# Gates of the attention heads: the sigmoid as exp(-ln(1 + exp(-x))) on ScalarE, the sum and the reciprocal on VectorE dropped

## The reference, cut to what matters

```
for layer in range(DEPTH):                       # DEPTH = 2
    h = rms_norm(x, norm_g[layer])
    proj = einsum('btd,dc->btc', h, w_in[layer])
    sb_q, sb_k, sb_v, sb_g, mb_q, mb_k, mb_v, mb_g, mem_q, mem_g = split(proj)
    o_sb  = merge_heads(stick_breaking_attention(...)) * silu(sb_g)    # 6 heads of 64
    o_mb  = merge_heads(moba_attention(...))           * silu(mb_g)    # 6 heads of 64
    o_mem = merge_heads(memory_attention(...))         * silu(mem_g)   # 4 heads of 64
    x = x + einsum('btc,cd->btd', concatenate([o_sb, o_mb, o_mem]), w_out[layer])
```

## Time and profile before

| | |
|---|---|
| three runs | 875.87, 870.71, 875.02 us |
| the profiled execution | 871.39 us |
| its span, first to last instruction | 869.5 us |
| TensorE (matmul) busy | 822.5 us, 95% |
| VectorE busy | 550.7 us, 63% |
| ScalarE busy | 471.6 us, 54% |
| GpSimd busy | 128.1 us, 15% |
| mean granted TensorE clock | 0.98 of full speed |

### The profile page before, as it was taken

One profiled execution on the slowest core, in us unless ns is written; L12 is line 12 of the kernel. 1 busy time (PEld: TensorE's weight loads), 2 busy tenths in 40 slices (PEclk: granted clock), 3 DMA queues, 4 the chain that ended last, 5 costly groups with the idle time before them and its releaser, 6 DMA issues.

```text
span 869.5 us, 12747 instructions
## 1 busy us (share of the span) xinstructions
PE 822.5 (95%) x4238; PEld 667.5 (77%) x4238; DVE 550.7 (63%) x797; ACT 471.6 (54%) x970; POOL 128.1 (15%) x205
## 2 busy tenths in 40 slices
PE   8998999999999999789998999999998999999996
PEld 5877877777776787587777888788886788888885
DVE  5567576676777776766665566666576455455444
ACT  5665665466775554645565656564546444344343
POOL 2100021000232210153323442200000000000000
PEclk9999999999999999998999999999999999999999
DMA  8964543366676454642223344456664556646641
GB/s 253 272 161 143 143 151 119 97 194 195 201 221 178 136 163 114 193 128 83 82 74 89 107 133 139 146 149 229 199 196 148 167 181 191 211 153 196 206 147 49
DMA packets 147454, 137.78 MB, mean 158 GB/s; under 512 B 15184, under 2 KB 115808, under 8 KB 147392
## 3 DMA queue, kind: packets, MB, share of 16 engines
q1 hardware_dynamic: 145296, 129.89, 49.4%
q0 software_dynamic: 2096, 7.09, 2.8%
HBM read 135.90 MB, written 1.05 MB: 157 GB/s over the span
## 4 chain that ended last, share of the span: by engine, by line
PE 73%; ACT 6%; DVE 4%; issue 2%; ACTq 0%; DVEq 0%
PE psum L1095 58%; PE psum L1061 6%; PE psum L1178 3%; PE psum L1313 2%; PE psum L1085 2%; ACT w_hi L1355 2%; ACT probs L1480 2%; PE psum L1281 1%; DVE w_lo L1548 1%; ACT p_t L1498 1%; DVE stats L1681 0%; PE psum L1239 0%; ACT gtmp L1523 0%; DVE x L1581 0%; ACT p_t L1366 0%
## 5 line engine op out<-in xcount | busy, mean ns | idle before, releaser
L1548 DVE TENSOR_TENSOR w_lo<-raw,w_hi 128x1024 fp32r<-128x1024 f32 (+1 forms) x254 | 296.7, 1184 | 134.5 <-ACT w_hi L1355 81.2
L1355 ACT ACTIVATE w_hi<-raw 128x1024 fp32r<-128x1024 f32 (+1 forms) x254 | 252.9, 1016 | 68.3 <-PE psum L1095 50.7
L1095 PE MATMUL psum<-w_hi,h_hi 128*128 128x512 f32 (+1 forms) x656 | 261.4, 398 | 10.3 <-DVE h_lo L1602 9.3
L1095 PE MATMUL psum<-w_lo,h_hi 128*128 128x512 f32 (+1 forms) x656 | 249.1, 380 | 0.0
L1095 PE MATMUL psum<-w_hi,h_lo 128*128 128x512 f32 (+1 forms) x656 | 248.7, 379 | 0.0
L1095 PEld LDWEIGHTS psum<-w_hi,h_hi 128*128 128x128 f32 x656 | 125.5, 191 | 35.6 <-issue 13.6
L1095 PEld LDWEIGHTS psum<-w_lo,h_hi 128*128 128x128 f32 x656 | 125.3, 191 | 19.6
L1095 PEld LDWEIGHTS psum<-w_hi,h_lo 128*128 128x128 f32 x656 | 125.9, 192 | 16.1
L1480 ACT ACTIVATE probs<-psum,stats 128x272 f32<-128x272 f32 (+2 forms) x104 | 47.3, 464 | 64.2 <-DVE stats L1673 27.9
L1095 PE MATMUL psum<-w_hi,m_hi 128*128 128x512 f32 x152 | 60.2, 396 | 2.4 <-DVE m_lo L1602 1.7
L1095 PE MATMUL psum<-w_lo,m_hi 128*128 128x512 f32 x152 | 59.3, 390 | 0.0
(11 more groups left out here) (175 smaller groups left out, 1042.0 us busy)
## 6 DMA issues: line engine op xcount, KB each, us to landing
raw<-in_w_in SPq DMA_DIRECT2D x112, 256.0 KB, 3.5
raw<-in_w_in SPq DMA_DIRECT2D x44, 512.0 KB, 4.3
raw<-in_w_ffn_in SPq DMA_DIRECT2D x88, 256.0 KB, 3.8
raw<-in_w_out SPq DMA_DIRECT2D x24, 512.0 KB, 3.3
raw<-in_w_in SPq DMA_DIRECT2D x64, 192.0 KB, 2.7
raw<-in_w_ffn_out SPq DMA_DIRECT2D x22, 512.0 KB, 4.6
raw<-in_w_mem_kv SPq DMA_DIRECT2D x8, 512.0 KB, 3.9
raw<-in_w_branch_swa SPq DMA_DIRECT2D x8, 512.0 KB, 3.4
```

The lines of the kernel that those rows point to most:

```text
L1095: last = nc.tensor.matmul(psum[:, bank, 0:n], sx[name][:, c, t * P:(t + 1) * P], wx[:, u["slot"], kk, 0:n], start=u["first"] and kk == 0 a ...
L1355: nc.scalar.activation(w_hi[:, u["slot"], :, 0:n], raw[:, u["raw"], :, 0:n], ACT.Copy)\
L1548: nc.vector.tensor_tensor(w_lo[:, u["slot"], :, 0:n], raw[:, u["raw"], :, 0:n], w_hi[:, u["slot"], :, 0:n].bitcast(F32), ALU.subtract)\
```

## The change

ScalarE now computes the whole sigmoid: exp(-x), then ln(1 + that) in place, then exp of its negative in place. The first two are each waited for by ScalarE before it issues the next. The signal `gate_e` moves to the third. VectorE is left with the multiplication by x. Semaphores, their counts, the order of steps and all else stay.

```diff
@@ ScalarE, step "gate"
                         act.wait_ge(gate_done, s["before"])
-                    nc.scalar.activation(gtmp[:, t, 0:gw], stage[:, g["ga"] % NSTAGE, t, c0:c0 + gw], ACT.Exp,
-                                         scale=-1.0).then_inc(gate_e, 1)
+                    gt = gtmp[:, t, 0:gw]
+                    link(nc.scalar.activation(gt, stage[:, g["ga"] % NSTAGE, t, c0:c0 + gw], ACT.Exp, scale=-1.0))
+                    link(nc.scalar.activation(gt, gt, ACT.Ln, bias=1.0))
+                    nc.scalar.activation(gt, gt, ACT.Exp, scale=-1.0).then_inc(gate_e, 1)
@@ VectorE, step "gate"
                     dve.wait_ge(gate_e, s["n"] + 1)
-
-                    gt = gtmp[:, t, 0:gw]
-                    link(nc.vector.tensor_scalar(gt, gt, 1.0, None, ALU.add))
-                    link(nc.vector.reciprocal(gt, gt))
-                    nc.vector.tensor_tensor(sgate[:, g["ga"] % 2, t, 0:gw], gt,
+                    nc.vector.tensor_tensor(sgate[:, g["ga"] % 2, t, 0:gw], gtmp[:, t, 0:gw],
                                             stage[:, g["ga"] % NSTAGE, t, c0:c0 + gw],
                                             ALU.mult).then_inc(gate_done, 1)
```

## The result

The full change was measured three times, each time beside the kernel before on the same chip:

| comparison | before, median (runs) | changed, median (runs) | ratio, 95% interval |
|---|---|---|---|
| first | 872.57 us (7) | 865.40 us (7) | 0.991, 0.9887 to 0.9934 |
| second (e12) | 874.91 us (25) | 867.21 us (6) | 0.9915, 0.9883 to 0.9946 |
| third (e16) | 873.54 us (23) | 865.40 us (6) | 0.991, 0.9883 to 0.9938 |

The account below looks back on a forecast made before the run. TensorE was taken to bound the kernel; waits of -1.64, -0.5 and -0.14 us and a clock drop of -1.7 us made -4.0 us, from a median of 875.02 to 871.0 us. Forecast 867 to 873 us, full range 865.5 to 877.5 us.

Parts of the forecast that it names:

- TensorE bounds the kernel, and only its waits can be given back: Between 30 and 338 us TensorE is busy 295.8 of 308 us, so at most 12.2 us can be given back directly.
- What leaves VectorE and what comes to ScalarE: Over 28 gates, additions and reciprocals of 37.3 us leave VectorE, and two more activations per gate bring ScalarE 19.9 us.
- ScalarE's side costs nothing: At the 28 gates, ScalarE's added 0.68 or 0.90 us each is covered by idle time and split-weight margins: 0 us.
- The wait until 266.35 and the clock drop behind it: TensorE's wait behind a 256-wide gate goes wholly, -1.64 us, and the half-clock stretch from 267.6 us with it, -1.7 us.
- next late is nothing near: After the wait until 266.35 goes, the high half behind the gate moves to 262.2, its unit unused until 272.8.
- The wait until 127.65: The chain behind the 256-wide gate at 116.92 to 119.49 starts earlier: -0.5 us, bounds 0 and -0.6.
- The wait until 70.66: TensorE's 2.28 us wait is set by ScalarE, despite two gates on VectorE ahead of it: -0.14 us.
- the sum: Gates between 30 and 336 us: three shorter waits give -2.3 us, with the clock drop -4.0 us.
- Nothing moves: The wait until 266.35 becomes another, or the clock drops elsewhere: 0 to -1.5 us, 873.5 to 875 us; chance 0.25.
- ScalarE becomes late: At gates without ScalarE idle time behind them, the added work reaches TensorE: slower, 878.5 us; chance 0.10.
- The tables are reloaded: On ScalarE each gate loads tables twice for ln and exp, 71.8 us; kernel near 900 us or more; chance 0.01.
- VectorE was late throughout: All eleven TensorE waits between 30 and 338 us, 12.2 us, and two clock drops go: 859.4 us; chance 0.07.

Follow-up runs that it names:

- e12: The full change, unchanged, for a second profile and more runs; 867.21 us, ratio to before 0.9915.
- e16: The full change, unchanged, measured beside the kernel of e15 on the same chip; 865.40 us, ratio to before 0.991.
- e2: Only the 24 128-wide gates computed on ScalarE, the four 256-wide as in the kernel before; 873.93 us, ratio to before 1.0002.
- e3: Kernel before with VectorE's addition and reciprocal left out and nothing added on ScalarE; 865.99 us, ratio to before 0.992.
- e4: Kernel before with the three activations on ScalarE, VectorE keeping addition, reciprocal and product; 877.16 us, ratio to before 1.0041.
- e9: Kernel before with one gate on ScalarE, the 256-wide one ahead of the wait until 266 us; 870.89 us, ratio 0.9961.
- e5: The kernel before, unchanged, for a second profile; 874.52 us, ratio to itself 1.0019.
- e6: Kernel before with only the first four gates, all 128 wide, computed on ScalarE; 872.65 us, ratio to before 0.9988.
- e10: The full change except the 256-wide gate ahead of the wait until 266 us, which stays on VectorE; 869.46 us, ratio to before 0.9944.
- e14: Kernel before with one gate on ScalarE, the 256-wide one at 116 us; 873.60 us, ratio to before 0.9998.
- e7: Kernel before with the four 256-wide and the first four narrow gates on ScalarE; 865.16 us, ratio to before 0.9919.
- e8: The full change plus the second pair of layer 0 memory transposes one unit earlier; 863.67 us, ratio to before 0.9899.
- e15: Same kernel as e8, measured again beside the unchanged full change on one chip; 864.82 us, ratio to before 0.9901.
- e11: The full change for all gates except the first four, which stay as before; 869.12 us, ratio to before 0.9933.
- e1: Kernel before with only the four 256-wide gates computed on ScalarE; 869.38 us, ratio to before 0.9959.
- e13: Kernel before with five gates on ScalarE, the first four and the 256-wide one ahead of the wait until 266 us; 869.25 us, ratio 0.9952.

## Why the prediction was right or wrong, point by point

**TensorE bounds the kernel, and only its waits can be given back: right.** VectorE lost 35 us and the kernel 7.7. With the waits moves the clock, on which more below. The 24 narrow gates, 29 us of VectorE's work (24 x 1.2), are worth nothing by themselves (e2: 1.0002).

**What leaves VectorE and what comes to ScalarE: right.** 37.3 and 19.9 us were forecast; in the window from 30 to 338 us VectorE is 32.9 us less busy and ScalarE 17.9 more. A little more of the program fits into the window after. The new rows add up to 15.0 us at 128 columns and 3.4 at 256, 18.4 us; the forecast's 19.9 has the links in it, in which the engine is not busy.

**ScalarE's side costs nothing: right as far as the times tell, but not for the reason given.** e3, without ScalarE's work, is no faster than the full change; its profile has 0.58 and 0.35 us less of two waits, so in the trace the added work is not quite free. The cover named was ScalarE's idle time and the margins of the split weights. e4 has both, adds the same work and is 3.6 us slower: the cover that counts is the work which VectorE no longer has behind the same gate.

**The wait until 266.35 and the clock drop behind it, -1.64 and -1.7 us: right that both go, and in part luck that their sum fits.** e9 changes that gate alone and gains 3.4 us (1.7 to 5.2 us) where the two terms make 3.3. In 18 profiles, seven have the wait (the first of before, e2, e4, e5, e6, e10, e14), each with one or two drops that begin between 266 and 274 us; eleven do not have it, and none of them has a drop between 262 and 280 us. Three of those (the first of after, e7, e12) have one at 284 to 286 us instead, behind waits that stayed there. So the drop goes with its wait, and can come back at a later one. The first profile of after is such a case. Windows, columns as in the earlier trace rows, of after and then of before:

```profile
284.50:287.90 3.40, 3.40 (x11) 2.74 (x11) 2.01 (x7) 0.53 (x2) 0.00 (x0) 0.50 0.81 224
```

```profile
465.60:469.00 3.40, 3.40 (x13) 2.96 (x11) 0.96 (x1) 1.93 (x3) 0.00 (x0) 0.50 0.02 5
```

Between 30 and 338 us both first profiles have two drops of 3.4 us, which the prediction had named as a sign of being wrong; the drop that after has fewer is the one at 465.6 us, where the change touches nothing. That the profiled execution came near the sum is therefore luck in its clock term. Nor is "next late is nothing near" right: TensorE's next wait, which ends between 279 and 293 us, is 0.27 to 0.30 us in five of the seven profiles with the drop at 266 to 274 us (0.53 and 0.99 in e6 and e4), and 0.63 to 0.99 us in ten of the eleven without (0.30 in e3).

**The wait until 127.65, -0.5 us: right in kind.** It is 0.74 us shorter in the full change, a little beyond the bound of 0.6, and 0.4 us by its own gate (e14).

**The wait until 70.66, -0.14 us: right.** 0.12 us. That the order sets it and not the gates held in e8 and e15.

**The step that failed is the sum, -2.3 us of waits and -1.7 us of clock.** It was made on one profiled execution and carried over to the median of the runs as it stood. It put the gates of 30 to 50 us at nothing, without a reason, and these carry a wait of 0.27 to 1.28 us in five of seven profiles. And it counted one clock drop of 1.7 us, where the runs show 4.6 us less withheld. These two are shown; how the whole 7.7 us divide is not.

*The missing term is the first four gates.* I said nothing of 30 to 50 us, since TensorE had no wait there in the one profile of before. The first weights are still landing then, and when they land varies. Where they land later, as in e11, the gate on VectorE follows the split at once and the stick-breaking sum is late. Of seven profiles with these gates on VectorE five have the early wait (1.28, 0.70, 0.54, 0.37 and 0.27 us; the first of before and e9 have not); of eleven with them off VectorE none has it. In the six in which these four gates are as before on both engines (all but e4) it follows the weights: the last high half ahead of them, which ScalarE begins when its weights are there, begins at 32.22, 32.27, 32.43, 32.94, 33.13 and 34.16 us, and the wait is 0, 0.27, 0, 0.37, 0.54 and 1.28 us. That the wait comes from these gates is shown; their price is 1.0 us from e6 and 1.9 us from e11 against e12, each of them with an interval that is as wide as the effect.

*The clock's term was 1.7 us, one drop.* Over all runs the mean granted clock was 0.9805 in the kernel before (100 runs, mean span 871.7 us) and 0.9857 in the full change (19 runs, 864.2 us). The clock withheld 17.0 and 12.4 us of the span, 4.6 us less, where one drop is 1.7. One gate alone, e9, has 3.0 us less withheld than before (1.5 to 4.5), e7 5.9 (4.0 to 7.8), e6 0.3 and e2 nothing. Within the runs of one kernel a microsecond withheld goes with a span longer by about 0.66 us, by a fit over all kernels' runs. By that the clock gives about 3 us of the 7.5 us in mean span, and waits and shifts the rest, 4.4 us, in place of 2.3; a fit is not an experiment, so that this division is an estimate. One reason why a drop costs less than what it withholds is in the profiles: the seven with a drop that begins between 168 and 175 us have 0.58 to 0.84 us of wait until 177 to 183 us, the other eleven 1.43 to 1.45 us. So a later wait takes back part of what the drop withheld. That makes 1.7 us too much for one drop, and too little for the clock in all. The one profile could not show either: at 869.5 us it was 2.2 us shorter than the mean span of its kernel, though its clock, 0.98, was the mean one. And the first profile of after was the second slowest of its seven executions.

**The rivals.** *Nothing moves* fell by its time (ratio 0.991), though what it named did happen in part: a drop elsewhere, and a next wait that grew. *ScalarE becomes late* fell for the full change. *The tables are reloaded* fell: the five loads of before are five after. *VectorE was late throughout* had a true part, the early gates, but for another reason than the eleven waits that I gave it.

**What stays open.** The parts make more together than apart. The 256-wide gates (3.6 us) and the narrow ones (0.0) add up to 3.6, and the full change gives 7.7; e7's eight gates give 7.1 where e1 and e6 add up to 4.6. The intervals of e1, e2 and the full change (about 1.5, 1.7 and, over three comparisons, 1.4 us to either side) do not close the first gap of 4.1 us. The second gap, of 2.5 us, is within the intervals of its three parts, and of e7's 5.9 us less withheld e1 has 3.3 and e6 0.3. e13 was additive, so it is not the first four with the one at 266. What makes the parts worth more together was not found. The profiles do speak against a gain after 338 us. TensorE's timeline at the last wait behind the gates, in the first profile of before, in e5, and in the first profile of after, e12 and e16:

```profile
341.94 0.47 PE L1095 MATMUL psum<-w_hi,mix_hi 128*128 128x512 f32 x1 [1.02 <-DVE mix_lo L1602]
345.83 0.47 PE L1095 MATMUL psum<-w_hi,mix_hi 128*128 128x512 f32 x1 [1.02 <-DVE mix_lo L1602]
339.32 0.77 PE L1095 MATMUL psum<-w_hi,mix_hi 128*128 128x512 f32 x1 [1.02 <-DVE mix_lo L1604]
340.14 0.70 PE L1095 MATMUL psum<-w_hi,mix_hi 128*128 128x512 f32 x1 [1.02 <-DVE mix_lo L1604]
338.43 0.47 PE L1095 MATMUL psum<-w_hi,mix_hi 128*128 128x512 f32 x1 [1.02 <-DVE mix_lo L1604]
```

The means are 343.9 and 339.3 us, 4.6 us apart. What follows this matmul takes 527.6 and 525.1 us before, and 526.7, 526.8 and 524.6 us after, 0.3 us apart in the mean. Five executions are few, but the gain that they show lies ahead of it.

## What to carry to other kernels

Moving work off an engine that is not the bound is worth the bound's waits that it ends and the clock that comes with them: here one gate of 28 holds almost half the gain (3.4 of 7.7 us) and 24 of them none by themselves. Before making a sum on a single profile, compare its time with the spread of the runs, take more than three runs for the base, and look at stretches where a slack is thin but no wait shows (here the start, where loads land at varying times). And price a wait of TensorE together with the drop of its clock that may follow, as here it did in seven of seven profiles.

## What the runs showed of the hardware

The same wait of 1.64 us was followed by a drop of the granted clock to 0.50, the level of 1.2 GHz, in all seven profiles that have it. The longer wait of 2.2 to 2.3 us until about 71 us was followed by one in nine of the sixteen that have it, and in neither of the two in which it is 0.55 us. So the length of the wait does not decide. Nor can the matmuls right behind it, since the sixteen profiles have the same program there. What does differ is the clock at the start: the seven without a drop near 72 us all show one that begins between 8 and 13 us, and of the nine with it eight show none there (e11 has both). Of the two with the short wait, e8 has no early drop and e15 has one. Why an early drop and the one near 72 us mostly exclude each other was not tested.

Two measurements of the identical program, pooled over 10 and 23 runs on one chip, differed by 0.19%, with an interval whose edge touches 1. Single executions of one kernel spread over 8 us (870.1 to 878.5 us in one set of 25 runs), and their granted clock goes with it.
